# Attention on one core: the low rotary product of two key pieces on 64 rows of TensorE each

## The reference, cut to what matters

```python
q = (rms_norm(c_q, g_cq) @ w_uq).reshape(B, L, 8, 128 + 64)
q_nope, q_rope = q[..., :128], q[..., 128:]
q_rope = apply_rope(q_rope, cos, sin)
k_rope = apply_rope(k_rope_raw, cos, sin)      # 64 wide, the same for all heads
s = (einsum('bqhd,bkhd->bhqk', qn, k_nope) + einsum('bqhr,bkr->bhqk', qr, k_rope)) * 192 ** -0.5
p = softmax(s);  out = p @ v
```

## Time and profile before

| | |
|---|---|
| median of 3 runs | 2153.77 us (2152.47 to 2154.11) |
| the profiled execution | 2151.28 us, span 2149.5 us |
| granted TensorE clock, mean | 0.998 |
| attention, with one or two heads in work | 936 to 1346 us |

### The profile page before, as it was taken

How to read it: one execution, slowest core, us unless ns; L and a number is a source line. 1 busy time by engine, 2 the same in 40 slices (tenths; PEclk the granted TensorE clock), 3 DMA queues, 4 the chain that set the end, 5 groups by cost and what they waited for, 6 DMA issues and landing times. The chain is left out here.

```text
span 2149.5 us, 32906 instructions
## 1 busy us (share of the span) xinstructions
PE 2100.0 (98%) x12560; PEld 1766.3 (82%) x12560; DVE 1282.6 (60%) x1967; ACT 947.8 (44%) x1550; POOL 397.3 (18%) x242
## 2 busy tenths in 40 slices
PE   8999999999999999989999999899999999999999
PEld 8988888788888887778888888777888888888886
DVE  3403665855856657447777778568766667552431
ACT  6314354453643544545555555545433323343422
POOL 1110000000000000111111111120154554424443
PEclk9999999999999999999999999999999999999999
DMA  5112122021111110221111110354322222344452
GB/s 190 60 55 68 37 65 69 32 67 59 49 59 44 64 60 30 90 99 45 46 45 44 44 44 25 123 205 137 118 87 81 89 79 93 131 161 164 157 180 94
DMA packets 79104, 181.87 MB, mean 85 GB/s; under 512 B 6976, under 2 KB 27776, under 8 KB 77344
## 3 DMA queue, kind: packets, MB, share of 16 engines
q1 hardware_dynamic: 79008, 180.56, 24.7%
HBM read 142.13 MB, written 38.40 MB: 84 GB/s over the span
## 5 line engine op out<-in xcount | busy, mean ns | idle before, releaser
L88 PE MATMUL h_bank<-hn_hi,w_hi 128*128 128x512 f32 (+2 forms) x952 | 371.5, 390 | 2.8 <-ACT raw L716 1.6
L90 PE MATMUL h_bank<-hn_hi,w_lo 128*128 128x512 f32 (+2 forms) x952 | 353.5, 371 | 0.0
L89 PE MATMUL h_bank<-hn_lo,w_hi 128*128 128x512 f32 (+2 forms) x952 | 352.9, 371 | 0.0
L88 PEld LDWEIGHTS h_bank<-hn_hi,w_hi 128*128 128x128 f32 x952 | 178.9, 188 | 33.2 <-issue 8.7
L90 PEld LDWEIGHTS h_bank<-hn_hi,w_lo 128*128 128x128 f32 x952 | 178.7, 188 | 28.3
L89 PEld LDWEIGHTS h_bank<-hn_lo,w_hi 128*128 128x128 f32 x952 | 179.2, 188 | 26.6 <-issue 3.8
L716 ACT COPY raw<-h_bank 128x512 f32<-128x512 f32 (+2 forms) x119 | 63.9, 543 | 264.3 <-PE h_bank L90 233.9
L2152 ACT CAST w_hi<-w_raw 128x1024 fp32r<-128x1024 f32 x79 | 82.8, 1049 | 213.6 <-PE f_bank L90 201.7
L1455 ACT CAST prob_hi<-a_bank 128x512 fp32r<-128x512 f32 x144 | 82.9, 588 | 130.7 <-PE a_bank L1723 130.2
L1134 POOL MEMSET ckv_hi<- 128x224 f32 x1 | 0.3, 284 | 757.1 <-POOLq L585 757.1
L2122 POOL TENSOR_TENSOR w_lo<-w_raw,w_hi 128x1024 fp32r<-128x1024 f32 x45 | 108.3, 2407 | 145.0 <-ACT w_hi L2152 145.0
(11 more groups left out here) (412 smaller groups left out, 5322.6 us busy)
## 6 DMA issues: line engine op xcount, KB each, us to landing
w_raw<-in_w_ffn SPq DMA_DIRECT2D x82, 512.0 KB, 3.8
w_raw<-in_w_hgrn SPq DMA_DIRECT2D x54, 512.0 KB, 3.4
raw_up<-in_w_ffn SPq DMA_DIRECT2D x18, 512.0 KB, 4.9
hidden<-gate_blocks SPq DMA_DIRECT2D x34, 256.0 KB, 2.0
w_raw<-in_w_out SPq DMA_DIRECT2D x15, 512.0 KB, 3.4
w_raw<-in_w_head SPq DMA_DIRECT2D x9, 512.0 KB, 6.0
X<-in_x SPq DMA_DIRECT2D x8, 520.0 KB, 9.0
values<-values_h SPq DMA_DIRECT2D x32, 128.0 KB, 1.7
```

The lines of the kernel that those rows point to most:

```text
L88: pe.matmul(out, wh, xh, start=start, stop=False)
L89: pe.matmul(out, wh, xl, start=False, stop=False)
L90: return pe.matmul(out, wl, xh, start=False, stop=stop)
```

## The change

The two low rotary products of a score head each use 64 rows in place of 128. A second copy of the high part of the rotary keys, `kr_again`, is kept in partitions 64 to 127. The low part of the queries is now in both halves of its partitions, so nothing is cleared. The first key piece is multiplied on partitions 0 to 63 (with `kr`), the second on partitions 64 to 127 (with `kr_again`), one instruction behind the other; both high products stand before them. The tail keeps its two products of 128 rows.

```diff
         self.table = sb("rope_table", [P, LP])[:, 0:L]
+        self.kr_again = sb("kr_again", [P, LP], F32R)
...
                         for x, (a, w) in enumerate(KEYS):
                             act.wait_ge(folded, x + 1)
+                            again = slice(P - ROPE, P)
+                            act.copy(lat.kr_again[again, key_at(a, w)], bank[x][again, 0:w])
                             act.copy(lat.kr[:, key_at(a, w)], bank[x][:, 0:w]).then_inc(hi_done["kr"], 1)
...
-                            sp.wait_ge(cleared, 4)
+                            sp.wait_ge(cleared, 2)
...
                 pool.wait_ge(cleared, 2)
-                for half in range(2):
-                    pool.memset(q_rope["lo", half][ROPE:P, :].bitcast(F32), 0.0).then_inc(cleared, 1)
-                pool.wait_ge(cleared, 4)
...
                 def fold_low(p, half):
                     fold_hi.wait(dve, p, half + 1)
-                    dve.tensor_tensor(q_rope["lo", half][0:ROPE, :], o_bank[0:ROPE, :],
-                                      q_rope["hi", half][0:ROPE, :].bitcast(F32), ALU.subtract
+                    dve.tensor_tensor(q_rope["lo", half][:], o_bank[:], q_rope["hi", half][:].bitcast(F32), ALU.subtract
                                       ).then_inc(fold_lo.sem, 1)
...
-                dve.wait_ge(cleared, 4)
+                dve.wait_ge(cleared, 2)
...
+                def rope_head(nxt, j, parts):
+
+                    x, i = nxt
+                    qs = slice(j * P, (j + 1) * P)
+                    for out, a, w in parts:
+                        pe.matmul(out, q_rope["hi", i][:, qs], kr[:, key_at(a, w)], start=False, stop=False)
+                    for (out, a, w), rows, keys in zip(parts, (slice(0, ROPE), slice(P - ROPE, P)), (kr, kr_again)):
+                        last = pe.matmul(out, q_rope["lo", i][rows, qs], keys[rows, key_at(a, w)], start=False, stop=True)
+                    return last
...
                     if j == 0:
                         fold_lo.wait(pe, x, i + 1)
-                    for part in parts:
-                        last = rope_terms(nxt, j, *part)
-                    last.then_inc(head_done.sem, 1)
+                    rope_head(nxt, j, parts).then_inc(head_done.sem, 1)
...
                     nope_terms((p, 0), 0, *second_part)
-                    for part in (first_part, second_part):
-                        last = rope_terms((p, 0), 0, *part)
-                    last.then_inc(head_done.sem, 1)
+                    rope_head((p, 0), 0, (first_part, second_part)).then_inc(head_done.sem, 1)
```

More of the change, by code:

```diff
@@ L1260, in attention_heads @@
         cq, ckv = ({x: lat.parts[n, x] for x in both_parts} for n in ("cq", "ckv"))
-        kr = lat.kr
+        kr, kr_again = lat.kr, lat.kr_again
         table = lat.table
```

## The result

The changed kernel takes 2164.68 us (median of 5 runs, 2163.02 to 2165.12), the kernel before in the same comparison 2152.47 us: a ratio of 1.0057, 95% interval 1.0046 to 1.0068. It is slower, by 12.2 us. In a second comparison the same kernel gave 1.0064 (1.0050 to 1.0077). Forecast were +16.8 us with a range of 2157 to 2179 us.

The account below looks back on a forecast made before the run. TensorE's instruction stream was taken to bound attention. 17.3 us for the visits net of the pairs' saving, less 0.5 hidden, plus 0 for other edits gave +16.8 us on 2153.77, so 2170.6 us, range 2157 to 2179.

Parts of the forecast that it names:

- TensorE's stream sets attention: Attention, 936 to 1346 us: TensorE busy 402.1 of 410.0 us, so changes to its stream arrive nearly one to one.
- The pair saves 0.125 us: Score heads: low products side by side hide the shorter one, 0.125 us less per head, 8.0 us over 64.
- Rival 3: Score heads: the second low product waits for the first, nothing is saved; 25.3 less 0.8 us hidden, 2178.3 us; 8%.
- A visit drains, and its first load is bare: Score heads: each change in or out costs about 0.10 us of draining and 0.11 us of uncovered weight load.
- Rivals 1 and 2: Score heads: 1, halves are no mode change, -8.0 us, 12%; 2, drain alone with next weights ready, +4.8 us, 10%.
- A visit costs 0.395 us: Score heads: one way in and out of 64 rows costs 0.395 us, read off L938; net 0.27 per head, 17.3 in all.
- At the start 0.5 us is hidden: Start of attention: waits for the exponentials hide the extra of one or two of four heads, 0.5 us off.
- The copies cost nothing: Values stage: three more ScalarE copies, 1.16 us, fit in ScalarE's idle; taken as 0, at most 1.2 us.
- a new wait of TensorE for ScalarE about 910 to 916 us: Values stage: named beforehand as a sign that the forecast was wrong; no size given.
- The other edits cost nothing: Dropped GpSimd clears and their waits, low split on 128 rows, tail's full-row products: each taken as 0 us.

Follow-up runs that it names:

- experiment 3: Changed kernel with both low products on rows 0 to 63, so they can't run side by side; 1.0095 of the kernel before.
- 7: Changed kernel with a third 64-row product of 240 columns, on rows 64 to 127, added to each visit, its result unused; 1.0070 of the kernel before.
- experiment 2: Changed kernel with the 512-column low product on 128 rows and the 272-column one alone on rows 0 to 63; 1.0099 of the kernel before.
- 4: Changed kernel with low products on rows 0 to 63 and the 272-column high product between them, two visits per head; 1.0202 of the kernel before.
- experiment 10: Kernel before with only the 16-row update (L938) put on all 128 rows, 112 of them zeros; 0.9984 of the kernel before, 2148.48 us.
- Experiment 8: Changed kernel with the last nope product of the second key piece (272 columns, 128 rows) moved behind the pair; 1.0071 of the kernel before.
- experiment 1: Changed kernel with both low products again on all 128 rows, one behind the other; 1.0012 of the kernel before.
- experiment 5: The changed kernel run again without any edit; 2165.28 us, 1.0064 of the kernel before.
- 6: Changed kernel with the three kr_again copies moved from unit 6 of the values stage to units 12 to 14; 1.0054 of the kernel before.
- experiment 9: Kernel before with both small recurrent products (16-column turn, 16-row update) put on the whole array; 0.9982 of the kernel before, 2148.27 us.

## Why the prediction was right, step by step

- *TensorE's stream sets attention.* Right. 12.8 us in 60 heads' streams, 13.0 us in all of attention.
- *The pair saves 0.125 us.* Right: starts 3 ns apart, 0.128 us less than the same two on one half (experiment 3), and the second half has room to spare (7). Rival 3 is out.
- *A visit drains, and its first load is bare.* Right in kind, and on the way in also in size: 0.22 us to the record of the first low product, 0.50 us its record, as forecast. Rivals 1 and 2 are out, by experiments 2, 4 and 10. The Trainium skill (TensorEngine Tiling (Array Packing), Key Properties) has the drain, and the trace agrees: each change holds the next load back by some 0.1 us (0.22 us in place of 0.12 on the way in). The bare load comes on top, 0.11 us in front of a common product and 0.06 in front of a transpose.
- *A visit costs 0.395 us.* This is the term that was mis-sized: it is 0.34 (experiment 2). The forecast took the way out from L938, which leads to L88, a common product with a load of 0.11 us. Behind a score head stand transposes, and their bare load takes 0.06 us. Experiment 8 puts a common product there and the 0.05 us come back. 60 x 0.05 = 3.0 us of the overshoot. At its own place the price read off L938 holds: 0.39 us (experiment 10). The length of these loads was there to be read: the transposes' is recorded with 0.14 us and a common one with 0.19, which is the same 0.05.
- *At the start 0.5 us is hidden.* In kind right: the first head's part, from attention's first product to its first transpose, is 36.29 us before and 36.53 after, +0.24 for four heads where 4 x 0.27 = 1.1 would stand if nothing were hidden. So 0.8 to 0.9 us are hidden at least; TensorE's idle there sinks from 2.10 to 1.79 us. But experiment 1, which makes no visit, has 36.48, and where the part has no stretch of lower granted clock it is 35.27 and 35.46 with visits (experiments 5 and 6) and 35.32 and 35.28 without (9 and 10). So nearly all of the 1.1 us seems to be hidden, twice what the forecast took off.
- *The copies cost nothing.* Wrong: 0.4 to 1.5 us (experiments 5 and 6), where the forecast allowed 1.2 at most. What it had named as a sign of being wrong, a new wait of TensorE for ScalarE about 910 to 916 us, is there: 0.34 us before 916.61 in experiment 5, and in the changed kernel's first execution a step of 0.42 in place of 0.23 us up to 912.00. The forecast looked at the idle in ScalarE and at how long TensorE's banks last, and left out that between the two stand the stores of the stage, for which ScalarE already waited.
- *The other edits cost nothing.* Nothing in the trace speaks against it; TensorE's waits for other engines in attention sum up to 7.4 us, and to 7.8 before. No run took one of these edits away by itself.

With the corrections the sum would be 60 x 0.213 + 0.24 + 0.4 to 1.5 = 13.4 to 14.5 us, or 0.2 less if the start hides all; the profiled execution is 13.6 longer in span, and the two comparisons measured 12.2 and 13.7. The 12.2 lies below that sum. A stretch of lower clock more or less in an execution, as the last section has it, would do that; that it did is not shown.

The mechanism was right and the number came out 3.1 to 4.6 us too high. It would have been further off but for some luck: the copies, taken at nothing, gave back 0.4 to 1.5 us of what the visit was overpriced.

Could a fuller visit win? Its second half has room for 240 more columns, such as most of a tail's low product. Even with both halves full it would save 0.23 us per head at most, and the visit costs 0.34. That is an estimate worked out from the rows; it wasn't tried.

## What to carry to other kernels

Half-empty rows of TensorE are no waste that packing recovers for nothing: in a stream of full products each visit to a part of its rows cost 0.34 to 0.40 us here (and the turn of 16 columns, experiment 9, 0.30), as much as one and a half products of 512 columns or more, so it takes more than that of columns run side by side in one visit to pay. Look for the opposite, too: a small product alone among full ones was quicker here when it was filled up with zeros to all rows, and that was the one kind of edit that made the kernel faster, by 0.16 to 0.18%. Price such a change by the starts of the records, and look at what load stands behind it.

## What the runs showed of the hardware that was not expected

- The bare weight load in front of a transpose takes 0.06 us and in front of other products 0.11 us (records of 0.14 and 0.19 us), with the same 128 columns: in the changed kernel the transposes' second load starts 0.06 us after the bare first one, and in experiment 3 the low products' second 0.11 us after it.
- Weight loads of the two row halves start 4 ns apart and both last 0.18 us: they don't queue behind each other.
- The same idle can cost a clock step or not. Two executions of the changed kernel have the same idle of 1.79 us at the first head's tail; in one the granted clock of 924 to 948 us was 0.94 (with a stretch at the lower level behind the idle), in the other 1.00, and the first head's part took 36.5 us in the one and 35.3 in the other. That moves an execution by about 1 us whatever the change does, in the kernel before too (0.94, 36.3 us): with the lower stretch the part takes 36.3 to 36.5 us in six of the twelve profiled executions, and 35.2 to 35.6 in the six without. What decides it is not shown. First the changed kernel, then its repetition (columns as in the earlier trace rows):

```profile
924.00:948.00 24.00, 20.89 (x95) 16.54 (x96) 10.79 (x18) 9.62 (x17) 5.32 (x4) 0.94 0.40 129
```

```profile
924.00:948.00 24.00, 20.48 (x98) 15.74 (x98) 10.84 (x19) 9.95 (x18) 5.32 (x4) 1.00 0.42 133
```
